# Index projections ahead of the queries, and the queries' rms moved into the softmax

## The reference, cut to what matters

```
q = rotary(rms_norm(q, q_norm_g)); k = rotary(rms_norm(k, k_norm_g))
qi, ki = rotary(qi), rotary(ki)
iscore[t,s] = sum_h wi[t,h] * relu(qi[t,h] . ki[s])      # 8 index heads of width 64
sel = top_k(iscore, 128)                                  # per query, causal by chunk
p = softmax(q . k / sqrt(128) over sel); attn = p . v     # 8 heads of width 128, 2 of k and v
```

## Time and profile before

| what | us |
|---|---|
| median of the runs shown | 3966.32 |
| lowest and highest of the three | 3965.72, 16569.1 |
| profiled execution, its own time | 3972.49 |
| its span, first to last instruction | 3970.7 |
| PE busy | 3596.8 (91%) |
| DVE busy | 2404.5 (61%) |
| ACT busy | 1094.6 (28%) |
| POOL busy | 2025.6 (51%) |
| mean granted TensorE clock | 0.949 of 2.4 GHz |

### The profile page before, as it was taken

The page is one execution under the profiler, slowest core; times in us unless marked ns, Lnnn a source line. Parts: engine busy times, 40 slices in busy tenths (PEclk is TensorE's granted clock), DMA queues, the critical chain, the costliest instruction groups (busy, mean ns, idle before and its releaser), DMA issues.

```text
span 3970.7 us, 50521 instructions
## 1 busy us (share of the span) xinstructions
PE 3596.8 (91%) x20020; PEld 3073.1 (77%) x20020; DVE 2404.5 (61%) x3010; ACT 1094.6 (28%) x1848; POOL 2025.6 (51%) x1100
## 2 busy tenths in 40 slices
PE   8899788999999989788899999999966767999998
PEld 7798678899999779666678888888755654578886
DVE  7786788774333867688966333333287883563335
ACT  4406432222210422633132220221033334322201
POOL 4254235466666535333556666666632442366664
PEclk9799899999999979899999999999977888999999
DMA  3122111122222312111222223222321112222232
GB/s 128 44 90 75 33 43 64 64 90 85 90 95 96 101 48 80 59 43 43 74 77 93 95 95 101 95 95 96 105 68 51 61 61 85 74 86 95 95 107 73
DMA packets 91424, 313.29 MB, mean 79 GB/s; under 512 B 10240, under 2 KB 12544, under 8 KB 91264
## 3 DMA queue, kind: packets, MB, share of 16 engines
q1 hardware_dynamic: 80064, 289.44, 22.1%
q10 hardware_dynamic: 11200, 21.71, 1.5%
HBM read 304.82 MB, written 6.29 MB: 78 GB/s over the span
## 4 chain that ended last, share of the span: by engine, by line
PE 65%; DVE 23%; ACT 9%; issue 3%; POOL 0%; DMA 0%; ACTq 0%; DVEq 0%; POOLq 0%
PE acc L448 19%; PE acc L449 19%; PE acc L451 18%; DVE cu L1727 7%; DVE trs L1598 2%; PE aux L594 1%; DVE rh L1685 1%; PE aux L662 1%; PE aux L741 1%; PE aux L677 1%; DVE w L1886 1%; DVE zz L2008 1%; PE acc L691 1%; ACT yv L1351 1%; DVE rb L1682 1%
## 5 line engine op out<-in xcount | busy, mean ns | idle before, releaser
L421 POOL TENSOR_SCALAR whi<-raw 128x1024 fp32r<-128x1024 f32 x548 | 616.9, 1126 | 1871.2 <-PE acc L451 1850.2
L423 POOL TENSOR_TENSOR wlo<-raw,whi 128x1024 fp32r<-128x1024 f32 x548 | 1408.8, 2571 | 45.7
L448 PE MATMUL acc<-nhi,whi 128*128 128x512 f32 (+1 forms) x2776 | 960.8, 355 | 92.8 <-DVE mt L1736 24.3
L449 PE MATMUL acc<-nlo,whi 128*128 128x512 f32 (+1 forms) x2776 | 953.0, 352 | 0.0
L451 PE MATMUL acc<-nhi,wlo 128*128 128x512 f32 (+1 forms) x2776 | 874.1, 350 | 0.0
L448 PEld LDWEIGHTS acc<-nhi,whi 128*128 128x128 f32 x2776 | 530.8, 191 | 179.5 <-issue 49.7
L449 PEld LDWEIGHTS acc<-nlo,whi 128*128 128x128 f32 x2776 | 530.2, 191 | 69.2
L448 PE MATMUL acc<-bhi,whi 128*128 128x264 f32 (+1 forms) x1864 | 561.9, 317 | 18.7 <-ACT rg L1077 11.7
L449 PE MATMUL acc<-blo,whi 128*128 128x264 f32 (+1 forms) x1864 | 546.2, 309 | 0.0
L451 PEld LDWEIGHTS acc<-nhi,wlo 128*128 128x128 f32 x2776 | 491.1, 191 | 69.4
L1727 DVE SCALAR_TENSOR_TENSOR cu<-cx,par,cu 128x528 f32<-128x528 f32 (+1 forms) x480 | 490.7, 1076 | 0.0
(11 more groups left out here) (359 smaller groups left out, 4745.5 us busy)
## 6 DMA issues: line engine op xcount, KB each, us to landing
raw<-in_w SPq DMA_DIRECT2D x548, 512.0 KB, 3.3
merge_gates<-gout ACTq DMA_DIRECT2D x16, 256.0 KB, 2.6
natab<-in_natab ACTq DMA_DIRECT2D x4, 896.0 KB, 7.4
h<-in_h ACTq DMA_DIRECT2D x8, 264.0 KB, 6.6
rope<-in_rope ACTq DMA_DIRECT2D x2, 1056.0 KB, 6.6
rnn_w<-in_gate ACTq DMA_DIRECT2D x2, 1024.0 KB, 9.5
sbc<-in_ssm ACTq DMA_DIRECT2D x4, 512.0 KB, 3.6
sg<-merge_gates ACTq DMA_DIRECT2D x8, 256.0 KB, 3.6
```

Source lines behind the costliest of these rows:

```text
L421: pool.tensor_scalar(hi, w, 1.0, 0.0, ALU.mult, ALU.add).then_inc(sem("w_hi"), 1)
L423: pool.tensor_tensor(lo, w, hi.bitcast(F32), ALU.subtract).then_inc(sem("w_split"), 1)
L448: pe.matmul(acc[s][:, f, 0:TH], hi, xh[:, f * TH:(f + 1) * TH], start=a, stop=False)
L449: pe.matmul(acc[s][:, f, 0:TH], hi, xl[:, f * TH:(f + 1) * TH], start=False, stop=False)
```

## The change

The three index query tiles are projected right after `vki`, then the two key heads, then the eight query heads; the phase `qk` becomes `kq`, and the weight order follows. Key heads keep their norm as it was. A query head keeps its rotation and loses root, reciprocal and product. The sum of its squares is formed the other way round: the squares are the stationary operand and one column of ones is the moving one, so the sum of each position lands on that position's partition, in one column per head and query group of `aux1` (columns from `QSUM` on). Five such products a head are issued in layer 0, four in layer 1. PE's index stage waits for five rotated tiles only (`15 * l + 5`), and issues the last head's sum behind its second product. After its last relu ACT takes the roots of all query sums at once (`std_q`), and DVE, in `choose` at n = 0, scales and inverts them into `qrs` (`query_scales`). In `mix` the scale 128^-0.5 of L1790 becomes 1, L1793 multiplies by `qrs` as well, and the exponential takes `qrs` as its scale per partition.

```diff
+QSUM = 128
-    PHASES += [(f"vki{_l}", 4, 1), (f"qk{_l}", 10, 1), (f"qi{_l}", 3, 1), ...
+    PHASES += [(f"vki{_l}", 4, 1), (f"qi{_l}", 3, 1), (f"kq{_l}", 10, 1), ...
-        src[b:b + 17] = [b + n for n in (10, 11, 16, 12, *range(10), 13, 14, 15)]
+        src[b:b + 17] = [b + n for n in (10, 11, 16, 12, 13, 14, 15, 8, 9, *range(8))]
...
+            def qk_sum(l, e):                                   # PE
+                T, o, it = LT[l], LO[l], l * 10 + e
+                pe.wait_ge(sem("qk_square"), it + 1)
+                if e < KV:
...
+                    for f in range(2):
+                        m = pe.matmul(aux[0][:, f, 0:T1 // 2], ones[:, :], tsq[:, e % 2, f * (T1 // 2):(f + 1) * (T1 // 2)],
+                                      start=True, stop=True)
+                else:
+                    for i in range(QT[l]):
+                        r, c = (P, META - o + i * P) if i < NQT else (META, 0)
+                        s = QSUM + i * HEADS + e - KV
+                        m = pe.matmul(aux[1][0:r, 1, s:s + 1], tsq[:, e % 2, c:c + r], ones[:, 0:1], start=True, stop=True)
+                m.then_inc(sem("qk_sum"), 1)
...
+                for e in range(3):
+                    tile(qi_, e, mine, T, each=("mix_lo", l * KD) if e == 0 else None)
                 for e in range(10):
-                    tile(qk, e, mine if e < 8 else normed, T if e < 8 else T1, each=("mix_lo", l * KD) if e == 0 else None)
+                    tile(kq, e, normed if e < KV else mine, T1 if e < KV else T)
                     if e:
-                        qk_sum(e - 1)
+                        qk_sum(l, e - 1)
...
             def index(l):                                       # PE
-                pe.wait_ge(sem("pj_done"), 15 * (l + 1))
+                pe.wait_ge(sem("pj_done"), 15 * l + 5)
...
+                        if (i, hh) == (0, 1):
+                            qk_sum(l, 9)
...
+                    if 1 <= e <= KV:                            # ACT, proj
+                        std_k(e - 1)
...
+            def std_q(l):                                       # ACT, behind the last relu of index
+                sums = aux[1][:, 1, QSUM:QSUM + (NQT + 1) * HEADS].rearrange("p (a b) -> p a b", b=HEADS)
+                if QT[l] > NQT:
+                    act.activation(qstd[0:META, NQT], sums[0:META, NQT], ACT.Sqrt, bias=EPS, scale=1.0 / HD)
+                act.activation(qstd[:, 0:NQT], sums[:, 0:NQT], ACT.Sqrt, bias=EPS, scale=1.0 / HD).then_inc(sem("q_std"), 1)
...
+                        if it == l * NQT * IXH:                 # ACT, index, ahead of the first relu
+                            act.wait_ge(sem("qk_sum"), 10 * (l + 1))
...
-                                   accum_out=rsum[0:r, b:b + 1]).then_inc(sem("at_exp"), 1)
+                                   scale=qrs[0:r, items[j][1], items[j][0]:items[j][0] + 1], accum_out=rsum[0:r, b:b + 1]).then_inc(sem("at_exp"), 1)
...
-                    if c == 2:                                  # DVE, turn
+                    if p not in (5, 6):
                         dve.tensor_tensor(dst, x, w, ALU.add).then_inc(sem("pj_done"), 1)
                         return
...
+            def query_scales(l):                                # DVE, in choose at n == 0
+                dve.wait_ge(sem("q_std"), l + 1)
+                if QT[l] > NQT:
+                    then(dve.tensor_scalar(qstd[0:META, NQT], qstd[0:META, NQT], float(HD) ** 0.5, None, ALU.mult))
+                    then(dve.reciprocal(qrs[0:META, NQT], qstd[0:META, NQT]))
+                then(dve.tensor_scalar(qstd[:, 0:NQT], qstd[:, 0:NQT], float(HD) ** 0.5, None, ALU.mult))
+                then(dve.reciprocal(qrs[:, 0:NQT], qstd[:, 0:NQT]))
...
-                    dve.tensor_tensor_reduce(sm[0:r, b, 0:W], src, add, float(HD) ** -0.5, CHOSEN, ALU.add, ALU.max,
+                    dve.tensor_tensor_reduce(sm[0:r, b, 0:W], src, add, 1.0, CHOSEN, ALU.add, ALU.max,
-                    dve.tensor_scalar(nmx[0:r, b:b + 1], mx[0:r, b:b + 1], -1.0, None, ALU.mult).then_inc(sem("at_max"), 1)
+                    dve.tensor_scalar(nmx[0:r, b:b + 1], mx[0:r, b:b + 1], -1.0, qrs[0:r, i, hh:hh + 1], ALU.mult, ALU.mult)\
+                       .then_inc(sem("at_max"), 1)
```

More of the change, by code:

```diff
@@ L1020, in proj @@
                     swap_quarters(p, T)
-                    if e == 0:
-                        std_qk(9)
+                for e in range(10):
+                    it, s, p = l * 10 + e, kq.slot(e), 15 * l + 5 + e
+                    T = T1 if e < KV else LT[l]
+                    block_done(kq.block(e) + 1)
+                    if e >= 2:
+                        act.wait_ge(sem("qk_sum"), it - 1)
+                    act.activation(halves(tsq[:, e % 2, 0:T], T), accv(s, T), ACT.Square).then_inc(sem("qk_square"), 1)
+                    act.wait_ge(sem("pj_done"), p - 1)
+                    x, w = tqg[:, (5 + e) % 2, 0:T], tsw[:, (5 + e) % 2, 0:T]
+                    act.activation(halves(x, T), accv(s, T), ACT.Copy, scale=col("k_g" if e < KV else "q_g", l))\
+                       .then_inc(evac[s], 1)
+                    act.wait_ge(evac[s], kq.nth(e) + 1)
+                    act.activation(w[0:64], x[64:128], ACT.Copy)
+                    act.activation(w[64:128], x[0:64], ACT.Copy).then_inc(sem("pj_swap"), 1)
+                    if 1 <= e <= KV:
+                        std_k(e - 1)
+                    if e == 3:
+                        act.wait_ge(sem("wi_turned"), l + 1)
+                        act.activation(wi[:, :, :], aux[1][:, 0, 0:NQT * 32].rearrange("p (a b) -> p a b", a=NQT)[:, :, 0:IXH],
+                                       ACT.Copy).then_inc(sem("wi_copied"), 1)
+            def std_q(l):
[3 more added lines that the diff above has]
+                act.activation(qstd[:, 0:NQT], sums[:, 0:NQT], ACT.Sqrt, bias=EPS, scale=1.0 / HD).then_inc(sem("q_std"), 1)
             def index(l):
@@ L1611, in proj @@
                 turn(1, qi[:, 0, LO[l]:], LT[l], LO[l], 2)
[L1612 to L1613 removed]
+                for e in range(3):
+                    turn(2 + e, qi[:, 1 + e, LO[l]:], LT[l], LO[l], 2)
                 for e in range(KV):
[L1615 to L1617 removed]
+                    turn(5 + e, k[:, e], T1, 0, 0)
+                for e in range(HEADS):
+                    turn(7 + e, q[:, e, LO[l]:], LT[l], LO[l], 0)
+            def query_scales(l):
[5 more added lines that the diff above has]
+                then(dve.reciprocal(qrs[:, 0:NQT], qstd[:, 0:NQT]))
             def index(l):
@@ L1707, in conv_inputs @@
                     choose(l, n)
+                    if n == 0:
+                        query_scales(l)
                 dve.sem_inc(sem("mask_done"), 1)
```

74 lines of the change are left out of this document (20 added, 54 removed).

## The result

| | us | runs |
|---|---|---|
| before, median | 3969.89 | 10 |
| after, median | 3958.06 | 10 |
| after, lowest and highest | 3956.39, 3961.30 | |
| after, profiled execution and its span | 3956.8, 3955.0 | |

One of the ten executions before took 16569.1 us; it is in the median of 3969.89, but not in the ratio. The ratio is 0.9975, 95% interval 0.9966 to 0.9984, which is 10 us (6 to 13); the two medians are 12 us apart. So the change makes the kernel 6 to 12 us faster. The forecast was a gain of 16.7 us, 3949.6.

The account below looks back on a forecast made before the run. DVE's reciprocal loop was taken to pace the head tiles, with PE close behind. Savings 1.35 + 3.0 + 6.0 + 6.3 = 16.7 us from 3966.3 gave 3949.6; own range 3942 to 3957, 8-in-10 range 3932 to 3961.

Parts of the forecast that it names:

- The new sum of squares: Head tiles: each query head's new sum on PE costs 1.4 us in layer 0, 1.2 in layer 1, at 0.15 a record.
- lower bound of 0.122: New sum of squares: least time per record in us, taken from PE's dense stretch of products.
- A stall of 0.3: Layer 0's head tiles: PE waits 0.3 us, as the third index tile needs an accumulator ACT reads when ki is rotated.
- of 1.2: Layer 1's head tiles: a stall of 1.2 us where the third tile waits for ACT, still copying v and ki.
- From the last tile to the steady index loop: Behind the last head tile: third relu at 6.1 us instead of 12.1 and 12.4, saving 6.0 and 6.3 us.
- I take the loop as cold, gain 0: Index loop: stays at the low clock after the change, so gains nothing.
- The rival that it runs warm: Index loop at full clock after dense tiles: 9.0 us a layer, 18 in all, 3931 us; chance 0.12.
- L1793 ... I take 0: Mixing: L1793's second operand costs between nothing and 0.02 us, times 72 items, up to 1.5 us; taken as 0.
- given back later: Rival: in mixing, more clock dips and 1.5 us of L1793 give back 9 us, 3958 us; chance 0.10.
- The sum: Total over both layers' head tiles and tails: 16.7 us gained, 3949.6 us on the median.
- the sum at 0.12 with DVE unheld: Fast end of the forecast's own range, 3942: sum of squares at 0.12 a record, DVE not held by POOL's subtraction.
- the same by 2%: Whole kernel: gain of 0.4%, below the 2% (79 us) told from no change; faster or slower by over 2%, 0.01 each.

Follow-up runs that it names:

- third trace: Profiled execution of the unaltered changed kernel in the last comparison, all four operand combinations on one chip; that run's median 3957.58 us, ratio 0.9970.
- stall run: Changed kernel with second and third index query tiles copied into idle buffers, and ACT's copy of the second moved ahead of v's: 3956.65 us, ratio 0.9968.
- fill run: Changed kernel plus nine unread 256-column products behind index products 0, 1 and 3 of the index loop's first group: 3950.74 us, ratio 0.9950.
- tail run: Changed kernel with the last head's rotation moved from before DVE's first index accumulation into the loop's last query group: 3954.44 us, ratio 0.9964.
- last medians: Second medians of the changed kernel with constant or per-partition operands, on one chip: 3950.39 neither dear, 3950.88 exponential, 3957.61 small instruction, 3957.58 both.
- last set: Changed kernel and its three constant-operand variants timed on one chip against the kernel before: ratios 0.9954 neither dear, 0.9961 exponential, 0.9972 small instruction, 0.9970 both.

## Why the prediction was right or wrong

**"The new sum of squares", 1.4 and 1.2 us: too dear.** Query head tiles follow each other at 6.97 us in layer 0, 5.87 of it dense, so 1.1; in layer 1 6.47 and 5.57, so 0.9. One sum in the trace, after:

```profile
140.39 1.08 PE L547 MATMUL aux<-ones,tsq 128*128 128x1 f32 x10
```

That is 0.11 a record, below the lower bound of 0.122 that I took from dense products of 264 columns. The products with v that I chose as nearest stream 128 columns. The Trainium skill, "TensorE: Matmul & The Clock Gate", section "LDWEIGHTS (loading the stationary operand)", gives 107 ns for a 128 column load (columns / 1.2 ns); the trace agrees with it, 0.108 a record. The estimate of 0.9 us a head from it was 0.2 too low in layer 0: the product with 16 columns, which layer 1 lacks, costs 0.2 as well. By this step alone the six sums ahead of the last tile cost 1.8 us less than forecast in each layer.

**"A stall of 0.3" and "of 1.2": 3.1 and 3.6.** This is the step that failed in the head tiles. From the marks, the second and third tile behind the first come after 7.02 and 7.83 us where a tile takes 5.87, 1.15 + 1.96 over; in layer 1, 1.1 + 2.5. (In the third trace layer 1's are 1.4 + 3.7.) So the wait that I named, of the third index tile, was right in layer 1 and too short in layer 0; the wait of the first key head behind it I did not have at all. What PE waits for, DVE and ACT in order of time:

```profile
64.88 0.39 PE L451 MATMUL acc<-bhi,whi 128*128 128x264 f32 x1 [0.91 <-ACT tqg L1006]
72.72 0.39 PE L451 MATMUL acc<-bhi,whi 128*128 128x264 f32 x1 [1.72 <-ACT tqg L1006]
```
```profile
65.89 2.79 DVE L1610 TENSOR_TENSOR qi<-tqg,tsw 128x528 f32<-128x528 f32 x1
...
68.78 0.61 ACT L1006 ACTIVATE tqg<-acc 128x528 f32<-128x528 f32 x1 [1.31 <-DVE qi L1610]
...
72.05 0.61 ACT L1006 ACTIVATE tqg<-acc 128x528 f32<-128x528 f32 x1
72.80 2.78 DVE L1608 TENSOR_TENSOR tsw<-tsw,rope 128x528 f32<-128x528 f32 x1
```

The first wait, 0.91 us, ends with a copy that ACT starts as soon as it is done copying v (64.25 us). The stall run, which puts this copy ahead of v's, has no such wait. The second, 1.72 us, ends with the copy at 72.05. Two things make it. I priced the held vector instruction (0.7 us that become 2.8 while POOL subtracts) in the tail and as a share of a head's period, and not here, where it holds ACT's copy at 68.78 and the swaps and the copy behind it. And that last copy is of the third index tile, which PE has just finished at 71.09: `slot(i)` is `i % 2` and each phase starts at `acc0` again, so behind the three tiles of `qi` the first key head takes the accumulator of the tile directly before it. The two are not used in turn at this seam, as the words on the kernel before have it. This is why the wait stays (1.9 us over a dense tile in place of 2.0) when the stall run's copies no longer wait for rotations. Letting `kq` start at the other accumulator would remove it; no run tries that. Together the two misses nearly cancel, which is luck: layer 0's tiles gave 0.3 and not 1.35, layer 1's 2.4 (0.9 in the third trace) and not 3.0.

**"From the last tile to the steady index loop", 6.1 us: right.** The third relus, after, in the chain of waits, stand 5.8 us behind their tile ends in both layers:

```profile
146.47 0.30 ACT tsq L1048
```
```profile
1399.27 0.30 ACT tsq L1048
```

The first rotation was held by POOL as foretold, 1.5 us in place of 0.7. Saved 6.3 and 6.7. With that rotation moved away, tail and loop are 2.9 and 2.1 us shorter still.

**"I take the loop as cold, gain 0": right for this kernel, and for the reason given, thin work and short waits ahead of it.** The rival that it runs warm did not come, but the fill shows how near it was: 10.2 us a layer, 8.7 without the convolution tile, where the rival had 9.0. The loop's own thin work does not make it cold: in the fill run it keeps 1.00 to its end. What decides is the clock at which PE enters the loop, and so the stretch directly behind the last head tile. The Trainium skill, the same page, section "Loop structure matters more than you think", shows a loop with a long DMA wait between its products as the one that goes cold, and one whose products follow each other at once as the one that stays warm. The fill run, 10.2 us a layer faster, agrees with it; in the tail run the clock fell with no wait above 0.45 us, so a long wait is not needed.

**"L1793 ... I take 0", and the exponential's operand, not named at all: this is the step that failed.** I put the second operand at 0 to 0.02 us with no row behind it. It takes 0.060 over the 0.154 of the earlier trace rows. The exponential of each item waits for it, on an engine that is busy 170 of the stage's 200 us. It cost 3.5 us in layer 0's mixing, and 7 us of the kernel by the last medians. The rival "given back later" named the place, this instruction and a clock that dips more, with a chance of 0.10. Its 3958 is the measured median to 0.1 us, and this is luck: it had 9 us given back where the traces have 3.5, with one stretched part more and not a handful of dips. The exponential's 0.092 us should have had a sentence and would have had the right answer for the wrong reason: ACT is busy 75 of 200 us there. The Trainium skill, "ScalarE: Activation LUTs", section "What ACT_TABLE_LOAD costs", has about 93 ns for each such operand; the trace agrees, 830 against 738 ns.

**The sum.** The two projections and index stages gave 16.0 us against 16.7 forecast, with a sum of squares too dear and a stall too short that hide each other. With both operands constant the kernel is 19.2 us below before in the last set, with them 12.0; the forecast missed by the give-back. Its own range, 3942 to 3957, is also wider than the two terms named for it: the sum at 0.12 with DVE unheld gives 3945, the sum at 0.18 gives 3953. The reading "the same by 2%" held.

## What to carry to other kernels

When a factor moves from one pass over a tile into an operand of a later instruction, price that instruction at the place where it now runs: 60 ns an item, 40 and 32 items in the two layers, undid a fifth of what the move won by the traces and over a third by the last medians. A reordering can be worth less than nothing alone and pay together with a shortening; ask what is queued last under each. Look up which buffer the first tile of a phase takes, above all behind a phase with an odd number of tiles. And before a loop of thin products is taken as slow by nature, look at the granted clock and the work just ahead of it: nine wasted products gave 10 us a layer.

## What the runs showed that I had not expected

- A vector instruction on one column takes 154 ns with an immediate, 214 with a per-partition operand, and 214 with both.
- Clock dips in a stage follow the program more than chance: the first two traces of the changed kernel have five in layer 0's mixing at the same offsets to 0.1 us (18, 45, 72, 123 and 150 us into it, in slices of 1.7 us). In the third the last one is at 176 and not 150. The number of long parts that they stretch, five, is the same in all three, and so is the stage's time.
- Slower exponentials made the stage faster: 194.2 and 194.5 us with the dear exponential, 196.5 and 196.9 with the cheap one. Three long parts are stretched in place of four, 1.5 us; why there is one less is open.
- The clock can fall while PE is busy with thin work (tail run, 8.35 of the 9 us from 141 to 150), and a loop of thin work can stay at the full clock (fill run, 1.00 from 151 to 171 us, PE busy 17.9 of 20).
